# Leaving out the matmuls of ones times the identity in a two-layer streaming encoder step

## What is computed

```python
h = x + 0.5 * rmsnorm(swiglu(rmsnorm(x, f1_pre), f1_up, f1_down), f1_post)
mix, new = token_mix(rmsnorm(h, m_pre), ...)      # four branches, gates, w_out
h = h + rmsnorm(mix, m_post)
h = h + 0.5 * rmsnorm(swiglu(rmsnorm(h, f2_pre), f2_up, f2_down), f2_post)
e = pe.astype(h.dtype) @ ple_w
h = h + rmsnorm(e * jax.nn.sigmoid(rmsnorm(h, ple_pre) @ ple_gate_w), ple_post)
```

## Time and profile before

| | |
|---|---|
| median of 3 executions | 3580.98 us |
| lowest and highest | 3574.42 and 3583.49 us |
| span of the profiled execution | 3572.6 us |
| mean granted clock over the span | 0.955 |
| PE busy | 3258.9 us (91%) |
| DVE, ACT, POOL busy | 1668.7, 612.0, 2049.9 us |
| records of line 539 | 528 on PE |

### The profile page before, as it was taken

How to read it: one execution, slowest core, us unless ns; L and a number is a source line. 1 busy time by engine, 2 the same in 40 slices (tenths; PEclk the granted TensorE clock), 3 DMA queues, 4 the chain that set the end, 5 groups by cost and what they waited for, 6 DMA issues and landing times. The chain is left out here.

```text
span 3572.6 us, 56188 instructions
## 1 busy us (share of the span) xinstructions
PE 3258.9 (91%) x23523; PEld 3097.6 (87%) x23523; DVE 1668.7 (47%) x1793; ACT 612.0 (17%) x1042; POOL 2049.9 (57%) x970
## 2 busy tenths in 40 slices
PE   7999997876999999999789999977589999999997
PEld 6999986775689899999789999867576999999997
DVE  4333154896366433312543321559944674333125
ACT  2010021012422210101221000200034222011021
POOL 6666763352156666677456677623422666666764
PEclk9999998988999999999989999989889999999998
DMA  3222221120112222232022222211211221222221
GB/s 92 81 81 82 81 62 43 41 74 27 43 57 79 60 77 82 81 88 77 15 82 81 82 81 83 60 39 37 66 45 30 67 77 54 82 82 87 82 68 39
DMA packets 455965, 236.27 MB, mean 66 GB/s; under 512 B 18630, under 2 KB 454150, under 8 KB 455814
## 3 DMA queue, kind: packets, MB, share of 16 engines
q1 hardware_dynamic: 445792, 227.05, 22.0%
q10 hardware_dynamic: 10022, 7.15, 0.6%
HBM read 228.53 MB, written 5.63 MB: 66 GB/s over the span
## 5 line engine op out<-in xcount | busy, mean ns | idle before, releaser
L1800 POOL TENSOR_TENSOR whi<-wraw,ones 128x1024 fp32r<-128x1024 f32 x432 | 826.2, 1912 | 1320.3 <-PE ps L522 1290.9
L1802 POOL TENSOR_TENSOR wlo<-wraw,whi 128x1024 fp32r<-128x1024 f32 x432 | 1094.1, 2533 | 34.0
L522 PE MATMUL ps<-u_hi,whi 128*128 128x288 f32 x4800 | 1063.9, 303 | 42.7 <-POOL u_lo L713 12.2
L522 PE MATMUL ps<-u_lo,whi 128*128 128x288 f32 x4800 | 1038.9, 298 | 0.0
L522 PE MATMUL ps<-u_hi,wlo 128*128 128x288 f32 x4800 | 1036.9, 297 | 0.0
L522 PEld LDWEIGHTS ps<-u_hi,whi 128*128 128x128 f32 x4800 | 779.3, 191 | 79.7 <-issue 36.1
L522 PEld LDWEIGHTS ps<-u_lo,whi 128*128 128x128 f32 x4800 | 779.9, 191 | 0.0
L522 PEld LDWEIGHTS ps<-u_hi,wlo 128*128 128x128 f32 x4800 | 778.5, 190 | 0.0
L760 DVE TENSOR_TENSOR sq<-sq,ps 128x576 f32<-128x576 f32 x88 | 66.3, 754 | 683.9 <-PE ps L522 683.9
L697 DVE TENSOR_TENSOR sqsum<-sqsum,sq 128x576 f32<-128x576 f32 x70 | 129.4, 1849 | 509.0 <-ACT sq L624 506.7
L522 PE MATMUL ps<-s_hi,whi 128*128 128x288 f32 x1408 | 303.8, 297 | 0.0
(11 more groups left out here) (276 smaller groups left out, 3127.4 us busy)
## 6 DMA issues: line engine op xcount, KB each, us to landing
wraw<-in_ffn_up SPq DMA_DIRECT2D x176, 512.0 KB, 3.8
wraw<-in_w_in SPq DMA_DIRECT2D x104, 512.0 KB, 3.8
wraw<-in_ffn_down SPq DMA_DIRECT2D x64, 512.0 KB, 3.9
wraw<-in_ffn_down SPq DMA_DIRECT2D x32, 384.0 KB, 3.3
wraw<-in_w_out SPq DMA_DIRECT2D x16, 512.0 KB, 3.8
wraw<-in_ple_gate_w SPq DMA_DIRECT2D x16, 512.0 KB, 3.8
wraw<-in_w_branch SPq DMA_DIRECT2D x16, 256.0 KB, 2.7
xtok<-in_x_prompt SPq DMA_DIRECT2D x4, 512.0 KB, 6.1
```

What stands on the lines that cost most here:

```text
L522: ins = pe.matmul(ps[:, 2 * p + f, 0:HT], wt[:, part, w], x[:, k, HT * f:HT * f + HT], start=start and n == 0 and c == 0, stop=stop and n ...
L1800: pool.tensor_tensor(whi[:, i_part, :], wraw[:, slot, :], ones[:, 0:1].to_broadcast([128, 1024]), ALU.mult).then_inc(w_rounded, 1)
L1802: pool.tensor_tensor(wlo[:, i_part, :], wraw[:, slot, :], whi[:, i_part, :], ALU.subtract).then_inc(w_split, 1)
```

## The change

The function `keep_clock` and its five call sites are deleted. Nothing else is edited; lines behind it move up (545 becomes 539, 555 and 556 become 548 and 549, 1670 becomes 1658).

```diff
-        def keep_clock(pe, n):
-            for _ in range(n):
-                pe.matmul(ps[:, 1, 0:128], ones[:], ident[:], start=True, stop=True)
...
         def pe_broadcast(pe, n):
-            keep_clock(pe, 3)
             pe.wait_ge(diag_ready, n + 1)
...
         def pe_norm_y(pe, n):
-            keep_clock(pe, 4)
             pe.wait_ge(sq_added, 8 * n + 8)
             token_sums(pe, sqsum, True, True).then_inc(norm_sum, 1)
             pe_broadcast(pe, n)
-            if n != N_F2POST:
-                keep_clock(pe, 14)
...
         def pe_norm_h(pe, n):
             for k in range(KD):
                 pe.wait_ge(sq_ready, 8 * n + k + 1)
                 token_sums(pe, sq[:, k % 2, :], k == 0, k == KD - 1, SAME).then_inc(sq_added, 1)
             pe_broadcast(pe, n)
-            keep_clock(pe, 6)
...
             if f == 0:
-                keep_clock(pe, 14)
                 pe_norm_y(pe, N_F1PRE)
```

## The result

The changed kernel takes 3623.37 us (median of 4 executions, 3608.28 to 3624.63) against 3580.83 us (median of 4, 3574.42 to 3583.49) for the kernel before. The ratio is 1.0112, 95% interval 1.009 to 1.0134: 1.1% slower, with 264 matmuls fewer. The profiled execution has a span of 3622.6 us, 50.0 more than that of before, and a mean granted clock of 0.931 against 0.955. PE is busy 17 us less in all, in a span that is 50 us longer.

A forecast was written before the change was run, and what follows sets the result against it. PE, busy for 91% of the span, loses time where it waits or runs at half clock. Terms sum to +42.4 us, added to the 3580.98 us median: 3623 us, 1.2% slower; range 3588 to 3642, own span 3608 to 3639.

The forecast's parts named there:

- sums of MPRE and F2PRE: Pre-norm sums in both layers: run at clock 0.50, 17.5 us in each of four places against 40.4 in all now, +29.6 us.
- their broadcasts: Broadcasts after the sums in MPRE and F2PRE: at half clock after the change, 4 x 1.1 = +4.4 us.
- broadcasts of F1POST, MPOST: Post-norm broadcasts: already at half clock wholly or in part, the rest adds 0 to 1, taken as +0.7 us.
- one-column sums of F1POST, MPOST: Post-norm sums: three of four at full clock now, some will be caught at half, a third taken, +0.9 us.
- first products after MPRE, F2PRE: Products behind these norms: start at half clock but wait for `u_lo`, slack hides some 2 us; +1 us for the four.
- F2POST and `ple_w`: F2POST's sums and broadcast and the first `ple_w` products: caught at half clock, 2.4 us a layer, +4.8 us (2.2 to 8).
- broadcast of PPRE: Broadcast behind PPRE's full-clock sums: at half clock in part, 0 to 1.1 us a layer, +1 us.
- the four places: Sign at MPRE and F2PRE of both layers: span from block end to first mixer product grows by 8 to 10 us each.
- the layer's edge: Sign at PPOST and F1PRE: they should look as before, with 0 us added.
- the sums themselves bring the clock back: Rival at MPRE and F2PRE: 3.9 us at half clock, then full clock; +11 us in all, 3592 us; chance 11%.
- the clock holds through the idle time: Rival: clock survives 11 us of little PE work before MPRE and F2PRE sums; 2.2 us come off, 3579 us; chance 4%.
- PPRE's sums at half clock: Rival: PPRE's sums behind the `ple_w` products are caught at half clock too, 8.3 us more a layer, 3640 us; chance 9%.

## Why the prediction was right, and where its terms were off

The forecast was 3623 us, 1.2% slower, by the loss of the clock in the sums of MPRE and F2PRE. The direction, the place and the mechanism were borne out: the stretches show the clock and the length of the sums, and the runs that put the groups of 14 back, leave them alone out or shorten the sums move the time as the clock and that length say. Term by term against the profile of before:

| term | forecast | measured in the trace |
|---|---|---|
| sums of MPRE and F2PRE | +29.6 | 4 x 17.42 - 40.4 = +29.3 |
| their broadcasts | +4.4 | 505.63 - 503.19 = 2.44 each, +4.4 |
| broadcasts of F1POST, MPOST | +0.7 | +0.7 |
| one-column sums of F1POST, MPOST | +0.9 | one of three at half clock, +0.8 (two of three in the second profile) |
| first products after MPRE, F2PRE | +1 | 0 |
| F2POST and `ple_w` | +4.8 | 0.9 + 0.8 a layer, +3.3 |
| broadcast of PPRE | +1 | 1.1 a layer, +2.2 |
| sum | 42.4 | 40.7 |

The value of 2.18 us for ten sums at half clock, taken from one-column sums, was the choice that carried the forecast; it measured 17.33 / 8 = 2.17. Ten sums of 1 column and of 64 take the same time at half clock, and PEld is busy for 17.1 of 17.2 us, which points to the weight load, the same in both, as what bounds them. The slack in the first products was real: they start at half clock (0.82 us for the first two records), fall up to 0.8 us behind, and have caught up with the sixth tile (6.42 us after the first record, before and after). The `ple_w` term was too high by 1.5 us: its sums never fell to half clock, and the products stood at 0.50 for 1.8 us only. PPRE's broadcast was too low by 1.2: it ran wholly at half clock in both layers. Of the signs named, the four places grew by 9.2, 9.6, 7.6 and 8.9 us, one a little under the 8 to 10 forecast, and the layer's edge, which was to look as before, took 2 us more.

**A step that was wrong without harm.** The sum was added to the median, "8.4 us above that span". The changed kernel's profiled execution took 3624.36 us with a span of 3622.6, 1.8 us more. So what lies around the span is some 2 us, and the profiled execution of before took about 3574.4, one of the quickest: most of the 8.4 us was that execution's distance from the median. Since the terms are differences, the median was the right base all the same. The spans differ by 50.0 us, 9.3 more than the terms measure: 4.6 in the first layer's mixer and 1.6 in the second's, 2.6 at the layer's edge, and small pieces. The second profile of before, against which the spans differ by 43.5 us, shows the first layer's part to be scatter of that kernel; for the second layer's, the run without the records around F2POST, in which the mixer and its norms are those of the kernel before, has 724.5 and 724.2 us in the two mixers where the changed kernel has 724.4 and 723.8. One of the changed kernel's four executions took 3608.28 us, 14 less than the next, and no profile says where. That the total was met to 0.4 us is therefore chance in part, and so is the sum of the terms, where errors of 1.0, 1.5 and 1.2 us partly cancel. The large term, right to 0.3 us, is not.

**The rivals.** That the sums themselves bring the clock back is refuted by 17.2 us of PE without a gap at 0.50, four times and again in the second profile. The row by which the prediction set this rival low said less than it was taken to say: the stretch from 1763.4 to 1770.1 ends where the clock rises, with PE, busy since 1763.2, in its group of 28 records, as the next stretch of that trace reads:

```profile
1770.10:1772.90 2.80, 2.80 (x25) 2.61 (x23) 2.80 (x5) 0.00 (x0) 1.86 (x1) 0.99 0.00 0
```

It shows sums, dummy matmuls and a broadcast at half clock for 6.7 us, and leaves open what longer sums would do; the changed kernel's rows decide it. The Trainium skill, page "TensorE: Matmul & The Clock Gate", section "What's actually happening", has sustained matmul activity release the throttle; the stretches of 17.2 us do not bear that out for matmuls of this kind, and the one-column dummies do not either. That the clock holds through the idle time is refuted by the same rows. PPRE's sums at half clock did not happen in the changed kernel; the run without 14 shows that they can.

## What to carry to other kernels

A matmul whose result nobody reads can pay for itself by what runs behind it, so before removing one, look at the granted clock of the next stretch and ask whether PE sets the pace there: the same half clock cost 8 us in each of the sums that PE bounded, and nothing in the first products of the mixer, which waited for other engines. Put such matmuls only there, and no more than it takes: 56 of 264 gave back nearly everything, and half-size groups did as well. Shortening the work that feels the clock did as much: with sums of half the length the changed kernel was as fast as the kernel before, though dummy matmuls still gained 8 us there.

## What the runs showed of the hardware

Occupation as the profile shows it is no sign of the clock: 28 one-column records kept PE and PEld busy for 5.80 of 5.80 us at 0.50, and 80 sums did so for 17.2 us.

Small DVE operations can take over ten times as long beside POOL's split of weights, 2.18 us instead of 0.16 for 128 x 2; around one such row an execution fell 2.2 us behind another of the same kernel. The Trainium skill, page "SBUF — State Buffer", section "SBUF: two separate sides", says that DVE, in an operation with two inputs in SBUF such as this one, and GpSimd share a pair of ports that whoever starts first holds for its whole instruction. The length agrees: POOL's split operations at that place take 1.89 and 2.34 us, and the DVE operation ends with one of them.
